# Expert gate and up products in three rounded matmuls, with their weights loaded apart from the down weights

## The chip, the cores and the metric

The kernel runs on one core of a Trainium2 chip. The metric is the time on the device, in microseconds (us), of one execution of the whole program. Engines are named as in the profile: TensorE (PE), ScalarE (ACT), VectorE (DVE), GpSimd (POOL) and SyncE (SP, which here only issues loads).

## The reference

Two transformer blocks over 256 tokens of width 1024, in float32. The first has latent attention, a causal convolution and a mixture of experts; the second has a gated delta rule layer and a forgetting-attention layer. Each layer is modulated by a vector, `ada = silu(c) @ ada_w + ada_b`, whose weights are large. The change touches the mixture of experts:

```python
for gi in range(N_GROUPS):                                   # 4 groups of 8 experts
    a = einsum('td,edf->tef', t, e_gate[gi])                 # d = 1024, f = 128
    u = einsum('td,edf->tef', t, e_up[gi])
    hid = silu(a) * u * combine[:, gi, :, None]              # combine: top 1 group, top 2 experts in it
    out = out + einsum('tef,efd->td', hid, e_down[gi])
```

## The kernel before

Each engine has a program of its own, and they meet at semaphores. `sig(name, events)` declares a semaphore with its events in order; `.then_inc(sig.up(key))` signals one, `e.wait_ge(sig, key)` waits for it.

**Weights** come in chunks, listed in the order of their loads by `chunks()` (L54), most of them 2048 columns of 128 partitions (1 MB). `ring_spots()` (L237) gives each chunk a place in one SBUF tensor, `ring`, of 26624 columns. SP issues the loads strictly in order (`load`, L3290), each after the chunks that lay in its place are freed (`before`, L252, and `freed_by`), and after the chunk eight places earlier in the list is freed. An expert's chunk has 3072 columns: 2048 of gate and up, 1024 of down. Between the experts lie 28 chunks of ada weights.

**The expert stage.** Tokens are routed on DVE (`route`), gathered by group with one-hot matmuls into `xg` (4 groups of 128 columns and a fifth for overflow), and then 40 units run: 32 experts and 8 overflow places, whose weights POOL fetches by indirect loads (`load_over`, L3087). TensorE's loop (from L1501) does in pass u: `up(u)` (L1051: 8 float32 matmuls, 128 tokens stationary, 256 columns of gate and up weights moving), `turn_hid(u-1)` (a transpose), `down(u-2)` (L1067: 2 float32 matmuls of 512 columns), a share of the ada columns, and in half of the passes a scatter of the previous group. The first passes also hold the weighing (`weigh`), the turning of the one-hots (`turn_pick`) and the gathering for the fifth group (`gather_over`). ACT does `silu_up(u)` and copies the transposed result; DVE (loop from L2980) does `gated_up(u)`, then its steps of ada work: each of 14 columns of 512 takes 8 instructions `acc += w[k] * c[k]` over two chunks, in 4 steps; one or two steps a pass,

```python
for _ in range((u + 1) * 7 // 5 - u * 7 // 5):
    next(gad, None)
```

then the scatter's additions to `xT`. POOL is idle in the stage but for the indirect loads, which it starts one after the other as places come free.

**Rounded products.** In most other projections a float32 product is made of three float32r products. A chunk in the list `SPLIT` is split in four pieces of 512 columns: ACT copies each, rounded, to `wH2` (`high`, L1568), and `wL2 = ring - wH2` is computed by POOL (`low`, L3060) or, where `by_dve` (L266) says so, by DVE. Both have two buffers of 2048 columns, so a chunk may be split once the chunk two before it in `SPLIT` was used. `split.need(name)` runs the splits up to that chunk at that point of an engine's program. The matmuls are `three` (L699): high by high, low weights by high, high weights by low. `xH2` and `xL2` hold the split tokens. `wH2`, `wL2`, `xH2` and `xL2` lie over columns 8192 to 20480 of `ring`, which the expert stage uses for chunks.

Of the kernel before, what the change touches and what calls it, by code (L numbers as in the profile page):

```python
# [17 lines left out]
RING = 20480  # L18
LONG = 26624
FIRST = 8192  # L20
LATE = 6144
NLOAD = 8
# [31 lines left out]
def chunks():  # L54
# [47 lines left out]
    for u in range(40):  # L102
        add(f"ex{u}" if u < 32 else f"ov{u - 32}", "expert", None, (0, 3072))
        while h < 28 and 10 * h <= 7 * u + 10:
# [34 lines left out]
def sizes():  # L139

    at, out = 0, {}
    for name, source, rows, cols in chunks():
        if source == "expert":
            out[name] = (0, 3072)
            continue
# [88 lines left out]
SPLIT = [n for n in ORDER if PLACE[n][1] == 2048 and n[:3] != "ada" and n[0] not in "uw"]  # L234


def ring_spots():  # L237
    out, at = {}, 0
    for name in ORDER:
        k = PLACE[name][1]  # L240
        at = {"ada3a": RING, "wob": 0, "ada4a": FIRST, "wout0a": 6144, "wout0b": 0, "ada7a": FIRST, "wout1a": 2048, "ada9a": 16384, "rt": RING + 1024, "ex0": 0, "ada1b": 4096, "ov6": LONG - 3072, "ada2_1_5b": 10240, "ov7": RING}.get(name, at)
        if at + k > (LONG if name in EARLY or "ex4" in out and name in WIDE else RING if name in WIDE else FIRST if "gt3b" not in out else LATE):
            at = 0
        out[name] = (at, at + k)
        at += k
# [6 lines left out]
def before(n):  # L252

    lo, hi = SPOT[ORDER[n]]
    if ORDER[n][:2] == "ov":
        out = [f"ov{int(ORDER[n][2:]) - 4}"] if int(ORDER[n][2:]) > 3 else []
    else:
        out = [m for m in ORDER[n % NLOAD:n:NLOAD] if m[:2] != "ov"][-1:]
# [7 lines left out]
def by_dve(name, q):  # L266

    if name[:2] in ("cv", "in") or name[0] in "ab":
        return q % 2 == 1
# [24 lines left out]
def build_program(nc, ins, out):  # L294
    ctx = ExitStack()
    with ctx:
# [22 lines left out]
        with ExitStack() as part:  # L319
            ring = part.enter_context(nc.sbuf_tensor("ring", [128, LONG], F32))  # L320
# [17 lines left out]
        with ExitStack() as part:  # L338
            sb1("ring_end", [128, LONG - RING])
            xg = sb1("xg", [128, 8, 640])  # L340
# [6 lines left out]
            silu = sb1("silu", [128, 2, 128])  # L347
            hid = sb1("hid", [128, 2, 128])
            hidT = sb1("hidT", [128, 2, 128])
            wsl = sb1("wsl", [128, 40])  # L350
        accs = [sz[:, 2 * i:2 * i + 2, :].rearrange("p i n -> p (i n)") for i in range(2)]
# [136 lines left out]
        norm_h = sig("norm_h", [(u, k) for u in (0, 2, 3) for k in K8])  # L488
# [29 lines left out]
        wo_p, wo_d = sig("wo_p", range(16)), sig("wo_d", range(16))  # L518
        yc_h = sig("yc_h", K8)
# [3 lines left out]
        wu_p = sig("wu_p", K8)  # L523
# [5 lines left out]
        hk_a, hk_d = (sig(n, [(h, q) for h in H2 for q in H2]) for n in ("hk_a", "hk_d"))  # L529
# [2918 lines left out]
```

## Time and profile before

| | us |
|---|---|
| median of 3 runs (lowest, highest) | 1166.06 (1163.05, 1166.13) |
| profiled execution | 1165.98 |
| its span, first to last instruction | 1163.9 |
| TensorE busy | 1091.4 |
| DVE, ACT, POOL busy | 627.6, 485.4, 394.3 |
| mean granted clock of TensorE | 0.975 |
| expert stage, first unit's matmul to last down product | 288.3 to 532 |

The page of the profile gives busy times over the whole span; stretches of it, called windows, are asked for by their start and end in us from the start of the span. Lines such as L687 are those of a helper that issues every matmul, so groups are told apart by their tiles: `bank<-ring,xg` is the gate and up product, `bank<-ring,hidT` the down product, `sz<-ring,cact,sz` an ada accumulation, `wL<-ring,wH` a low piece of a split.

### The profile page before, as it was taken

The page shows a single profiled execution, that of the slowest core. Times are in us where ns is not written, and L with a number is a line of the kernel's source. Part 1 is how long each engine was busy: PE and PEld are TensorE (multiplying, and loading weights), DVE is VectorE, ACT ScalarE, POOL GpSimd, SP SyncE. Part 2 cuts the span into 40 slices and gives each one's busy share as a digit, 9 for nine tenths or more (in the row PEclk, how much of TensorE's full clock was granted, in tenths as well). Part 3 has the DMA queues.
Part 4 walks back from the last instruction along what each step waited for, and adds up shares of the span by engine and source line. Part 5 has one row for each costly group of instructions (what it writes and reads, how often), then busy time and mean ns, then how long its engine had stood idle before and what let it go on. Part 6 is the DMA issues. An engine that isn't in the chain of part 4 may idle for free. (4 is left out here: it accounts for less than half of the span.)

```text
span 1163.9 us, 20437 instructions
## 1 busy us (share of the span) xinstructions
PE 1091.4 (94%) x8310; PEld 930.1 (80%) x8310; DVE 627.6 (54%) x1369; ACT 485.4 (42%) x1091; POOL 394.3 (34%) x337
## 2 busy tenths in 40 slices
PE   5989979999989999999989999999899989999996
PEld 2787778888767777776878889899788878788875
DVE  5789862864425455454654535634554353454473
ACT  3433444304101101104575865746734544465543
POOL 0541342100000000112584563555442436455431
PEclk9999989999999999999999999999999998899999
DMA  9524324587499999604222322232211223233311
GB/s 365 220 104 180 108 74 157 193 361 308 169 381 376 391 394 398 228 14 183 73 109 75 109 74 74 73 110 77 106 38 39 90 94 120 99 109 125 130 37 37
DMA packets 25869, 186.25 MB, mean 160 GB/s; under 512 B 4144, under 2 KB 4912, under 8 KB 5680
## 3 DMA queue, kind: packets, MB, share of 16 engines
q1 hardware_dynamic: 24192, 184.77, 41.5%
q8 instruction: 66, 1.08, 0.4%
q10 hardware_dynamic: 432, 0.18, 0.1%
q14 instruction: 27, 0.22, 0.1%
q0 software_dynamic: 1152, 0.00, 0.1%
HBM read 196.46 MB, written 1.05 MB: 170 GB/s over the span
## 5 line engine op out<-in xcount | busy, mean ns | idle before, releaser
L3058 POOL TENSOR_TENSOR wL<-ring,wH 128x512 fp32r<-128x512 f32 x210 | 277.7, 1336 | 304.9 <-ACT wH L1566 304.4
L687 PE MATMUL bank<-xH,wH 128*128 128x256 f32 x832 | 260.5, 313 | 16.1 <-DVE xL L2195 7.1
L687 PE MATMUL bank<-xH,wL 128*128 128x256 f32 x832 | 240.1, 289 | 0.0
L687 PE MATMUL bank<-xL,wH 128*128 128x256 f32 x832 | 239.8, 288 | 0.0
L687 PEld LDWEIGHTS bank<-xH,wH 128*128 128x128 f32 x832 | 164.0, 197 | 33.3 <-issue 13.7
L687 PEld LDWEIGHTS bank<-xH,wL 128*128 128x128 f32 x832 | 164.5, 198 | 4.9 <-issue 4.3
L687 PEld LDWEIGHTS bank<-xL,wH 128*128 128x128 f32 x832 | 163.9, 197 | 0.0
L1566 ACT ACTIVATE wH<-ring 128x512 fp32r<-128x512 f32 x264 | 154.5, 619 | 8.6 <-PE bank L687 5.4
L687 PE MATMUL bank<-ring,xg 128*128 128x256 f32 x640 | 145.5, 381 | 3.5 <-DMA ring<-in_exw 3.5
L687 PEld LDWEIGHTS bank<-ring,xg 128*128 128x128 f32 x640 | 119.5, 190 | 26.2 <-DMA ring<-in_exw 7.0
L2195 DVE SCALAR_TENSOR_TENSOR sz<-ring,cact,sz 128x512 f32<-128x512 f32 x154 | 118.4, 769 | 4.3
L1566 ACT ACTIVATE arena<-bank 128x512 f32<-128x512 f32 (+5 forms) x133 | 67.3, 511 | 123.8 <-PE bank L687 98.2
L3092 POOL DMA_INDIRECT ring<-in_exw,small x8 | 8.2, 1020 | 275.9 <-DVE sz L2195 242.1
L1563 ACT ACTIVATE silu<-bank 128x128 f32<-128x128 f32 x40 | 11.1, 278 | 199.7 <-PE bank L687 199.7
L687 PE MATMUL bank<-arena 64*64 64x64 f32 (+5 forms) x1056 | 81.7, 252 | 6.2 <-DVE arena L2192 4.9
L2195 DVE SCALAR_TENSOR_TENSOR arena<-bank,vec,arena 128x255 f32<-128x255 f32 (+2 forms) x96 | 46.1, 481 | 66.1 <-ACT arena L1566 63.7
L687 PEld LDWEIGHTS bank<-arena 64*64 64x64 f32 (+4 forms) x1056 | 66.6, 154 | 18.8 <-issue 12.8
L687 PE MATMUL bank<-arena,ring 128*128 128x256 f32 (+2 forms) x336 | 75.5, 381 | 1.5 <-POOL arena L3243 1.2
L2195 DVE SCALAR_TENSOR_TENSOR hid<-silu,wsl,bank 128x128 f32<-128x128 f32 x40 | 13.8, 347 | 115.6 <-ACT silu L1563 110.1
L687 PE MATMUL bank<-ring,hidT 128*128 128x512 f32 x160 | 75.1, 593 | 0.0
L2195 DVE SCALAR_TENSOR_TENSOR arena<-arena,vec 128x256 f32<-128x256 f32 (+1 forms) x132 | 65.9, 566 | 12.9 <-ACT arena L1563 12.9
L687 PEld LDWEIGHTS bank<-arena,ring 128*128 128x128 f32 (+2 forms) x336 | 60.0, 181 | 14.0 <-POOL arena L3243 2.0
(213 smaller groups left out, 1850.5 us busy)
## 6 DMA issues: line engine op xcount, KB each, us to landing
ring<-in_wts SPq DMA_DIRECT2D x123, 1024.0 KB, 5.1
ring<-in_exw SPq DMA_DIRECT2D x32, 1536.0 KB, 9.2
ring<-in_wts SPq DMA_DIRECT2D x1, 1152.0 KB, 5.2
xT<-in_xT SPq DMA_DIRECT2D x1, 1024.0 KB, 13.4
out<-hT SPq DMA_DIRECT2D x4, 256.0 KB, 2.5
cst<-in_cst SPq DMA_DIRECT2D x1, 800.0 KB, 6.3
ring<-in_wts SPq DMA_DIRECT2D x1, 640.0 KB, 3.7
vec<-in_vec SPq DMA_DIRECT2D x1, 217.0 KB, 5.7
```

The source lines that it names most:

```text
L687: return pe.matmul(o, l, r, start=start, stop=stop, skip_group_check=True)
L1563: return act.activation(o, a, func, scale=scale, bias=bias)
L1566: return act.activation(o, a, ACT.Copy, scale=scale)
L2195: return dve.scalar_tensor_tensor(o, a, s, b, op0, op1)
L3058: return pool.tensor_tensor(o, x, h.bitcast(F32), ALU.subtract)
L3092: pool.indirect_dma_start(raw(name)[:, 0, :], None, ins["exw"], bass.IndirectOffsetOnAxis(ap=rowi[:, j:j + 1], axis=0), bounds_check=4095, ...
```

## The change

- `up` uses rounded products: the chunk's two halves by the group's split tokens. The chunk of an expert is cut in two, `ex` (gate and up, 2048 columns) and `dn` (down, 1024 columns). `ex` and `ov` chunks go into `SPLIT`.
- In the list of loads `ex` runs three units ahead of `dn`, and the ada chunks come two to three units later than before.
- In the stage `ring` has four expert places of 3072 columns and two ada places of 2048, outside `wH2` to `xL2`. The first three overflow chunks go over `xg` and what follows it (columns 28672 to 37888).
- A load waits for the chunk twelve places earlier to have landed, no longer for one eight places earlier to be freed.
- ACT and DVE get `group(t, h)`: the high and the low part of half of group t's tokens. The ada steps on TensorE and DVE begin with pass 2.
- POOL runs the splits of the stage, and waits in `load_over` between them. Several semaphores are merged.

```diff
     for u in range(40):
-        add(f"ex{u}" if u < 32 else f"ov{u - 32}", "expert", None, (0, 3072))
-        while h < 28 and 10 * h <= 7 * u + 10:
+        for n in range(3 if u else 0, 4):
+            if u + n < 32:
+                add(f"ex{u + n}", "expert", None, (0, 2048))
+        if u < 32:
+            add(f"dn{u}", "expert", None, (2048, 3072))
+        else:
+            add(f"ov{u - 32}", "expert", None, (0, 3072))
+        while h < 28 and 10 * h <= 7 * u - 3:
...
-SPLIT = [n for n in ORDER if PLACE[n][1] == 2048 and n[:3] != "ada" and n[0] not in "uw"]
+SPLIT = [n for n in ORDER if n[:2] == "ov" or PLACE[n][1] == 2048 and n[:3] != "ada" and n[0] not in "uw"]
+def expert_spots():
+    four = (0, 3072, RING, RING + 3072)
+    out = {f"ex{u}": four[u % 4] for u in range(32)}
+    out.update((f"dn{u}", four[u % 4] + 2048) for u in range(32))
+    out.update((f"ov{j}", (LONG, LONG + 3072, LONG + 6144, *four, LONG)[j]) for j in range(8))
+    for n in ORDER[ORDER.index("rt"):ORDER.index("gqk0a")]:
+        if n[:3] == "ada":
+            out[n] = 6144 if n[-1] == "a" else RING + 6144
+    return {**out, "gqk0a": 0, "gqk0b": 6144, "ba": 2048}
...
 def by_dve(name, q):
-    if name[:2] in ("cv", "in") or name[0] in "ab":
+    if name[:2] == "ex":
+        return q == 3 and name != "ex0"
+    if name[:2] in ("cv", "in", "ov") or name[0] in "ab":
         return q % 2 == 1
...
             def up(u):
-                t, w = u // 8, raw(expert(u))
-                p = bank(u % 2)
-                e.wait_ge(loaded(expert(u)), expert(u))
+                t, name = u // 8, expert(u)
+                wh, wl = parts(name, 8)
+                p = bank(u % 2)[:, 0:256]
+                c = slice(128 * (t % 2), 128 * (t % 2) + 128)
                 for k in range(8):
-                    e.wait_ge(*((xg_a, k) if t < 4 else (pick_a, "o1")))
-                    i = mm(p[:, 0:256], xg[:, k, 128 * t:128 * t + 128], w[:, 0, 256 * k:256 * k + 256], k == 0, k == 7)
+                    e.wait_ge(lo_of(name, k // 2), (name, k // 2))
+                    e.wait_ge(hk_d, ("g", t, k // 4))
+                    mm(p, xH2[:, k, c], wh[:, k, :], k == 0, False)
+                    mm(p, xH2[:, k, c], wl[:, k, :], False, False)
+                    i = mm(p, xL2[:, k, c], wh[:, k, :], False, k == 7)
...
-                for _ in range((u + 1) * 7 // 5 - u * 7 // 5):
+                for _ in range((u - 1) * 7 // 5 - (u - 2) * 7 // 5 if u >= 2 else 0):
                     next(gad, None)
...
+            def group(t, h):
+                if t >= 2:
+                    e.wait_ge(up_p, 8 * t - 9)
+                if t == 4:
+                    e.wait_ge(pick_a, "o1")
+                else:
+                    e.wait_ge(xg_a, 4 * h + 3)
+                s, c = slice(4 * h, 4 * h + 4), 128 * (t % 4)
+                cp(xH2[:, s, 128 * (t % 2):128 * (t % 2) + 128], xg[:, s, c:c + 128]).then_inc(xg_a.up((t, h)))
...
             high_tokens()
+            split.need("ex0")
             gather()
+            group(0, 1)
+            split.need("ex1")
             for u in range(42):
                 if u < 40:
                     silu_up(u)
...
                 if 1 <= u < 41:
                     turn_hid(u - 1)
+                if u < 38:
+                    split.need(f"ex{u + 2}" if u < 30 else f"ov{u - 30}")
+                if u % 8 in (2, 3) and u < 32:
+                    group(u // 8 + 1, u % 8 - 2)
...
             route()
             gad = chain(*[ada(j) for j in range(10, 24)])
+            group(0, 0)
+            group(0, 1)
+            split.need("ex1")
             for u in range(42):
...
                 if 1 <= u < 40:
                     gated_up(u)
-                for _ in range((u + 1) * 7 // 5 - u * 7 // 5):
-                    next(gad, None)
+                if u >= 2:
+                    for _ in range((u - 1) * 7 // 5 - (u - 2) * 7 // 5):
+                        next(gad, None)
+                if u < 38:
+                    split.need(f"ex{u + 2}" if u < 30 else f"ov{u - 30}")
+                if u % 8 in (2, 3) and u < 32:
+                    group(u // 8 + 1, u % 8 - 2)
...
-            e.wait_ge(rt_d, "rowi")
-            for j in range(8):
-                load_over(j)
+            for u in range(40):
+                split.need(f"ex{u}" if u < 32 else f"ov{u - 32}")
+                if u == 28:
+                    e.wait_ge(rt_d, "rowi")
+                    for j in range(3):
+                        load_over(j)
+                if 31 <= u < 36:
+                    load_over(u - 28)
...
+                for m in [m for m in ORDER[n % NLOAD:n:NLOAD] if m[:2] != "ov"][-1:]:
+                    e.wait_ge(loaded(m), m)
                 for m in before(n):
```

## Rows read from the trace of the kernel before

**Rows 1.** The page, part 1: busy us (share of the span) xinstructions.

```profile
PE 1091.4 (94%) x8310; PEld 930.1 (80%) x8310; DVE 627.6 (54%) x1369; ACT 485.4 (42%) x1091; POOL 394.3 (34%) x337
```

**Rows 2.** Windows of the expert stage (first line: columns).

```profile
core 0: us, PE busy (x) PEld busy (x) DVE busy (x) ACT busy (x) POOL busy (x), PEclk, DMA share, GB/s
302.30:367.80 65.50, 61.20 (x279) 45.70 (x278) 25.20 (x45) 8.00 (x27) 0.00 (x0) 1.00 0.86 345
367.80:474.10 106.30, 106.30 (x475) 80.42 (x474) 52.76 (x100) 10.18 (x40) 2.21 (x2) 1.00 0.97 390
474.10:526.70 52.60, 52.60 (x235) 39.81 (x234) 25.58 (x52) 5.09 (x20) 5.95 (x6) 1.00 0.30 104
500.00:520.00 20.00, 20.00 (x93) 15.50 (x92) 9.20 (x19) 1.33 (x6) 3.35 (x4) 1.00 0.02 1
```

**Rows 3.** Waits of TensorE, 296 to 365 us: total, times, longest.

```profile
PE bank L687 <- DMA ring<-in_exw: 3.5, 3, 1.9
```

**Rows 4.** Timeline of TensorE: start us, us, what; the transposes of passes 2 and 39.

```profile
302.28 0.27 PE L691 MATMUL bank<-cst,hid 128*128 128x128 f32 x1
...
526.69 0.27 PE L691 MATMUL bank<-cst,hid 128*128 128x128 f32 x1
```

**Rows 5.** Timeline of TensorE, gate and up products; windows of the last projections.

```profile
288.27 7.07 PE L687 MATMUL bank<-ring,xg 128*128 128x256 f32 x32
967.55:973.30 5.75, 5.75 (x48) 5.75 (x49) 1.02 (x2) 2.34 (x5) 5.75 (x7) 1.00 0.52 184
```

**Rows 6.** Tile ring: duration ns min/median/max; then timelines of POOL and DVE.

```profile
L1566 ACT ACTIVATE wH<-ring x264: 612/617/648, 24.7 to 1146.6; 128x512 fp32r<-128x512 f32 x132
L3058 POOL TENSOR_TENSOR wL<-ring,wH x210: 1252/1289/1791, 25.4 to 1146.5; 128x512 fp32r<-128x512 f32 x105
L2192 DVE TENSOR_TENSOR wL<-ring,wH x54: 674/692/1782, 28.3 to 1147.2; 128x512 fp32r<-128x512 f32 x54
...
31.54 3.38 POOL L3058 TENSOR_TENSOR wL<-ring,wH 128x512 fp32r<-128x512 f32 x2 [1.42 <-ACT wH L1566]
31.38 4.09 DVE L2192 TENSOR_TENSOR wL<-ring,wH 128x512 fp32r<-128x512 f32 x3
...
539.08 2.35 DVE L2192 TENSOR_TENSOR wL<-ring,wH 128x512 fp32r<-128x512 f32 x2
```

**Rows 7.** Groups of DVE, 367.8 to 474.1 us: busy us, mean ns.

```profile
L2195 DVE SCALAR_TENSOR_TENSOR sz<-ring,cact,sz 128x512 f32<-128x512 f32 x45 | 33.7, 750 | 1.2
L2195 DVE SCALAR_TENSOR_TENSOR xT<-bank,adaT,xT 128x256 f32<-128x256 f32 x20 | 8.7, 478 | 1.9 <-PE bank L687 1.7
L2198 DVE TENSOR_SCALAR sz<-ring,cact 128x512 f32<-128x512 f32 x7 | 3.4, 480 | 0.0
```

**Rows 8.** DMA, 368 to 474 us.

```profile
DMA packets 4671, 41.41 MB, mean 391 GB/s; under 512 B 772, under 2 KB 772, under 8 KB 772
q1 hardware_dynamic: 4388, 41.33, 96.8%
```

**Rows 9.** Timelines of DVE and TensorE at the start of the stage.

```profile
293.05 0.48 DVE L2198 TENSOR_SCALAR sz<-ring,cact 128x512 f32<-128x512 f32 x1
295.17 2.29 PE L687 MATMUL bank<-small,pick 128*128 128x8 f32 x20
298.22 0.33 PE L691 MATMUL bank<-cst,hid 128*128 128x128 f32 x1 [0.76 <-DVE hid L2195]
```

**Rows 10.** Windows, columns as in rows 2.

```profile
536.00:539.30 3.30, 1.71 (x11) 1.10 (x10) 3.25 (x9) 3.30 (x8) 3.30 (x4) 1.00 0.00 0
539.40:542.80 3.40, 3.40 (x8) 2.70 (x9) 2.03 (x2) 1.18 (x4) 3.40 (x3) 0.50 0.51 173
```

**Rows 11.** Timelines at the end of the stage; the page, part 6: KB, us to landing.

```profile
527.47 1.53 DVE L2195 SCALAR_TENSOR_TENSOR sz<-ring,cact,sz 128x512 f32<-128x512 f32 x2
534.66 4.27 ACT L1566 ACTIVATE wH<-ring 128x512 fp32r<-128x512 f32 x8
535.03 0.36 PE L687 MATMUL bank<-pickT,ysH 128*128 128x256 f32 x1
...
ring<-in_wts SPq DMA_DIRECT2D x123, 1024.0 KB, 5.1
```

More of the change, by code:

```diff
@@ L18 @@
 RING = 20480
-LONG = 26624
+LONG = 28672
+OVER = 37888
 FIRST = 8192
 LATE = 6144
-NLOAD = 8
+NLOAD = 12
 BIG = 1.0e30
@@ L143, in sizes @@
         if source == "expert":
-            out[name] = (0, 3072)
+            out[name] = (0, cols[0][1] - cols[0][0])
             continue
@@ L254, in before @@
     lo, hi = SPOT[ORDER[n]]
[L255 to L258, printed above, removed]
+    out = []
     for m in range(n - 1, max(-1, n - 40), -1):
@@ L319, in build_program @@
         with ExitStack() as part:
-            ring = part.enter_context(nc.sbuf_tensor("ring", [128, LONG], F32))
+            ring = part.enter_context(nc.sbuf_tensor("ring", [128, OVER], F32))
         sb("ring_start", [128, LATE])
@@ L487, in build_program @@
         norm_a = sig("norm_a", [(u, k) for u in G4 for k in K8])
-        norm_h = sig("norm_h", [(u, k) for u in (0, 2, 3) for k in K8])
+        norm_h = sig("norm_h", [(u, k) for u in range(4) for k in K8])
         hi_a = sig("hi_a", [(n, q) for n in SPLIT for q in G4])
@@ L528, in build_program @@
         hk_p = sig("hk_p", H2)
-        hk_a, hk_d = (sig(n, [(h, q) for h in H2 for q in H2]) for n in ("hk_a", "hk_d"))
+        hk_a = sig("hk_a", [(h, q) for h in H2 for q in H2])
+        hk_d = sig("hk_d", [(h, q) for h in H2 for q in H2] + [("g", t, h) for t in range(5) for h in H2])
         rt_p, rt_d = sig("rt_p", ["lg", "rank"]), sig("rt_d", STEPS)
@@ L598, in ada_name @@
             return f"ada{j}" if j < 12 else f"ada2_{j // 6 - 2}_{j % 6}"
-        def under_split():
-            names = [n for n in WIDE if SPOT[n][0] < RING and 12288 < SPOT[n][1]]
-            return [freed_by([n for n in names if (n[:3] == "ada") == x][-1])[0] for x in (False, True)]
         def used(name):
             x = 2 * (name[-1] == "b") + 1
+            if name[:2] in ("ex", "ov"):
+                return up_p, int(name[2:]) + 32 * (name[0] == "o")
             if name[:2] == "cv":
@@ L647, in ahead @@
                 for _ in range(n):
-                    if i < len(SPLIT) and self.n < 4 * i + 4 and SPLIT[i][:4] != "gqk0":
+                    if i < len(SPLIT) and self.n < 4 * i + 4 and SPLIT[i][:2] not in ("ex", "ov") and SPLIT[i][:4] != "gqk0":
                         self.go()
@@ L1026, in gather_over @@
                 m.then_inc(pick_p.up(f"o{i}"))
-                until(7, (pick_a, f"o{i}"))
+                until(2, (pick_a, f"o{i}"))
             def weigh():
@@ L1067, in down @@
             def down(u):
-                t, w = u // 8, raw(expert(u))
+                t, name = u // 8, f"dn{u}" if u < 32 else f"ov{u - 32}"
+                w = raw(name)[:, 0, -1024:]
+                e.wait_ge(loaded(name), name)
                 e.wait_ge(ht_a, u)
```

119 lines of the change are left out of this document (66 added, 53 removed).

## The prediction, made before the changed kernel was run

> **What bounds the kernel now.** I read the page first, then the stage of the experts by windows, then its engines one by one. TensorE is busy for 94% of the span [rows 1], so the page alone says that TensorE bounds the kernel. The expert stage runs from 288 to about 533 us. In its middle TensorE was busy for all 106.3 us, at full clock, and the DMA engines for 0.97 of it, while POOL had nothing to do but two gathers [rows 2]. Two limits therefore lie on top of each other. Only in the first 65.5 us did TensorE wait: 4.3 us were not busy, of which 3.5 us were waits for expert weights [rows 2, 3].
>
> The stage has a simple clock. In pass u TensorE does the gate and up products of unit u, the transpose for unit u-1, the down product of unit u-2, then a share of the ada columns and of the scatter. The transpose's one matmul marks the pass: the marks at 302.28 and 526.69 [rows 4] are passes 2 and 39, and the windows of rows 2 are cut at such marks: 10 passes in 65.5 us, 18 in 106.3 (5.91 each), 9 in 52.6.
>
> **The products.** A unit's gate and up product is 8 float32 matmuls of 256 columns, recorded as 16; 32 of them take 7.07 us, less the tail of the last (0.17), so 0.216 us each and 3.45 a unit [rows 5]. The change makes 24 float32r matmuls of 256 columns. The trace has the same shape in the last projections: 48 in 5.75 us, 0.12 us each [rows 5], so 2.88 a unit. TensorE gains 0.576 us a pass, 5.8 in the first ten, 10.4 in the middle 18 and 5.2 in the last 9. I take this as firm.
>
> **What must now be made.** Each unit's 2048 columns are rounded by ACT in four pieces of 0.617 us (2.5 a unit, and ACT is 10% busy) and subtracted in four pieces: three on POOL (1.289 each, 3.9 a unit), one on DVE (0.692 at the median) [rows 2, 6]. For the eight overflow units it is two and two. The token halves cost an ACT and a DVE instruction of 512 elements for each half of each group of 8 units, ten in all. DVE's own work in the middle 18 passes is 52.8 us [rows 2], of which 45 accumulations and 7 first products of ada columns, all with SBUF sources, are 37.1 and the scatter's additions, from PSUM, 8.7 [rows 7]. It grows by 18 x 0.69 = 12.4 and some 4.5 x 0.69 = 3.1, to 68.3 us. That would hide in 95.9 us of TensorE if DVE and POOL did not disturb each other.
>
> They do. Where both subtract back to back, POOL's two took 3.38 us and DVE's three 4.09; at 539 us DVE's two took 2.35 [rows 6]. A pair in turns costs about 1.7 us, against 1.29 and 0.69 alone. So a POOL instruction holds up DVE by between 0 (DVE is idle or works from PSUM just then) and 1.0 us (1.7 - 0.69). With 54 of them in 18 passes DVE needs between 68.3 and 122 us. I take 0.6, since DVE's accumulations come in runs of two or four inside POOL's run of three but scatter and gating work lies between: 68.3 + 32.4 = 100.7 us.
>
> The Trainium skill (SBUF — State Buffer, "SBUF: two separate sides") calls the pair of ports that DVE and GpSimd share an exclusive lock, held for the whole instruction, against a DVE instruction with two SBUF inputs. By that rule a pair costs the sum of both, 1.98 us, and the middle passes at least 54 x 1.289 plus 37.1 of ada work plus 15.5 of new subtractions, 122 us: an estimate that falls on the far end of my range. The trace agrees that the two hinder each other, but its pairs take 1.7 us, less than the rule gives [rows 6].
>
> **DMA.** The 18 passes moved 41.41 MB at 391 GB/s with the queue at 96.8% [rows 8]. At 100% that is 41.41/0.404 = 102.5 us for the same weights. The change moves the same bytes, so this too ends the middle part later than TensorE (95.9). The smaller ring (four expert places and two ada places, 16384 columns instead of 26624) is covered as long as a chunk may be late by some 10 us: an expert's chunk is free once it is split, two passes ahead of its use, instead of after the down product.
>
> So the middle part: the last of 95.9 (TensorE), 100.7 (DVE) and 102.5 (DMA): 102.5, a gain of 3.8 where TensorE alone would give 10.4. The first ten passes have little ada and scatter work; there TensorE's 5.8 and the 3.5 of waits come off, 9.3 together, since gate and up chunks are now asked for before the stage begins instead of after the first down product. In the last nine DMA is no limit (104 GB/s [rows 2]); DVE's need is 25.6 + 16 x 0.69 + 16 x 0.6 = 46.2 us of 47.4 left by TensorE. POOL now waits there for down products ahead of its splits, and each overflow load costs it about 1 us (5.95 for six [rows 2]). I take 4.5 of the 5.2.
>
> **What the change adds at the start.** Unit 0 used to begin at 288.27, beside DVE's routing. Now it waits for the low halves of the tokens, which DVE subtracts only after its routing ended at 293.05 [rows 9]: begin at 294.0 (one subtraction and two semaphores), units 0 and 1 in 5.8, to 299.8. The weighing (20 small matmuls from 295.17, then 0.8 of waiting until 298.22 [rows 9]) takes 3.05 as before, to 302.9, and unit 2 ends at 305.8 instead of 301.8: +4.0. Bounds: 2.5, if DVE is let off earlier, and 5.5. TensorE idles for 5.7 us meanwhile. At 536 to 539.3 it was busy for 1.71 of 3.3 us, and then ran 3.4 us at 0.50 of its clock, 1.2 GHz [rows 10]. I add such a stretch, 1.7 us; bounds 0 and 3.4.
>
> **At the end.** The ada steps begin two passes later. Before, two steps (four accumulations, the first two from 527.47 in 1.53 us) followed the last gating; now five do, 7.7 us, and the last chunk is only asked for when its place is freed in the first of them, 5.1 us before it lands [rows 11]. The last group's low half, and with it the last scatter (535.03 [rows 11]), is late by the three steps more less some 2.3 us in which DVE used to idle there (2.3), or by the landing and two steps (4.3). The splits for the next projection (534.66, 4.27 us of ACT) wait for a load from the same queue. I take 3.0.
>
> Costed at nothing: the merged semaphores, the wait for a landing in place of a freeing among the early loads (it lets some ada chunks come sooner, but DVE there waits ahead of other work that TensorE paces), unit 0's own split (5.2 us of POOL, which is idle then, beside the gather; without that cover unit 0 would begin that much later, but it has to wait for DVE until 294 anyway), and the overflow loads, which transfer nothing here (two of them ran at 500 to 520 us, where DMA moved 1 GB/s [rows 2]).
>
> **Sum**, against the profiled execution's 1165.98 us (span 1163.9 and 2.1 around it; the median of the runs shown, 1166.06, is the same): +4.0 +1.7 -9.3 -3.8 -4.5 +3.0 = -8.9, so 1157 us.
>
> **Rivals.**
> - A, TensorE keeps its pace. Chunks loaded ahead cushion DMA and DVE slips between POOL's instructions: 5.7 - 9.3 - 10.4 - 5.2 + 2.3 = -16.9, 1149 us. For it: DVE has 30 us of room if POOL costs it nothing, and POOL itself needs only 3.9 us a pass. Against it: DMA at 0.97 [rows 2]. Chance 0.25.
> - B, slower: DVE and POOL in turns bound the stage. If each POOL instruction costs DVE 1.0, the middle takes 122.2 us (+15.9), the first ten 25.2 + 8.4 + 30 = 63.6 (-1.9), the last nine 52.5 (-0.1); with start and end 5.7 + 4.3 that is +23.9, 1190 us. The forecast turns into it at about 0.75 us a POOL instruction, where the whole change is worth nothing. For it: the pairs of rows 6, and that ada accumulations come back to back. By the Trainium skill's rule of the lock (SBUF — State Buffer, as above) the middle would take about the same. Chance 0.27.
> - C, the smaller ring starves the queue. A stuck ada load holds SP, and behind it the experts' loads: at 90% of the queue's time instead of 96.8% the middle takes 114 us, +7.7 instead of -3.8: about +3, 1169 us. For it: an ada chunk waits for DVE to free one two chunks back. Against it: expert chunks have two passes of room. Chance 0.1.
> - That nothing changes because the new products don't run is excluded: 24 matmuls replace 16 in every unit.
>
> The forecast's own case has 0.38; its range with start, end and DVE's 0.5 to 0.7 is 1151 to 1164.
>
> **How the numbers follow.** A measurement tells about 0.3% (3.5 us) of this kernel from no change. Faster: all of A, 0.28 of the forecast's 0.38 and little of C, 0.54. Same: 0.07 of the forecast, 0.05 of B, 0.03 of C, 0.15. Slower: the rest, 0.31. The range goes from A's value less the clock's 1.7 (1147) to B at 0.9 us a POOL instruction (1180); B's far end is left out.
>
> **What would show it.** Right: matmuls of 0.12 us in the stage, marks of 5.7 us in the middle with the DMA share at 0.95 or more, POOL at some 70%, TensorE idle from 288.3 to 294, no wait for expert loads before 345 us. If DVE's accumulations average over 1.1 us and TensorE waits for DVE's low pieces or gating, B holds; if marks are 5.3 us, A; if the DMA share falls while SP waits for an ada place, C. The prediction is wrong at its root if the stage is paced by something with no term here, such as ACT waiting ahead of the splits.

## The result: 1.7% slower, and where the profile shows it

The changed kernel took 1184.91 us at the median of four runs (1183.32 to 1186.62) beside 1165.72 for the kernel before: a ratio of 1.017 (95% interval 1.0149 to 1.0191), 19 us more. The forecast was 1157, with a range up to 1180. The profiled execution has a span of 1183.5 us.

The same windows, cut at the same marks, carry the reading. Part 1 of the page after the change, then the timeline of TensorE at the transposes of passes 2, 28, 29, 30 and 39 ("start us, us, what"):

```profile
PE 1080.0 (91%) x8630; PEld 933.7 (79%) x8630; DVE 743.5 (63%) x1426; ACT 574.3 (49%) x1261; POOL 566.0 (48%) x450
...
316.53 0.27 PE L708 MATMUL bank<-cst,tmpb 128*128 128x128 f32 x1
...
467.52 0.30 PE L708 MATMUL bank<-cst,tmpb 128*128 128x128 f32 x1
...
481.71 0.41 PE L708 MATMUL bank<-cst,tmpb 128*128 128x128 f32 x1
...
487.92 0.27 PE L708 MATMUL bank<-cst,tmpb 128*128 128x128 f32 x1
...
543.25 0.27 PE L708 MATMUL bank<-cst,tmpb 128*128 128x128 f32 x1
```

The windows of the changed kernel, with the columns of [rows 2]: ten passes, eighteen, nine.

```profile
316.50:375.90 59.40, 55.30 (x359) 45.05 (x358) 53.07 (x53) 31.03 (x71) 49.05 (x31) 1.00 0.86 336
375.90:487.90 112.00, 99.70 (x611) 80.06 (x610) 100.35 (x123) 50.66 (x116) 86.80 (x58) 0.97 0.89 353
487.90:543.20 55.30, 49.53 (x307) 40.31 (x306) 52.98 (x72) 21.57 (x52) 28.07 (x21) 0.97 0.40 144
```

| part | before | after | forecast | found |
|---|---|---|---|---|
| to the mark of pass 2 | 302.3 | 316.5 | +5.7 | +14.2 |
| first ten passes | 65.5 | 59.4 | -9.3 | -6.1 |
| middle 18 | 106.3 | 112.0 | -3.8 | +5.7 |
| last nine | 52.6 | 55.3 | -4.5 | +2.7 |
| the rest | 637.2 | 640.3 | +3.0 | +3.1 |

TensorE does less work (PE 1080.0 against 1091.4 [rows 1]) and waits more. In [rows 2] it was busy for all 106.3 us of the middle, now for 99.7 of 112. DVE rose from 52.8 to 100.4 us and POOL from 2.2 to 86.8. The groups of DVE and POOL in the middle passes (busy us, mean ns) say what DVE's time is:

```profile
L2237 DVE SCALAR_TENSOR_TENSOR sz<-ring,cact,sz 128x512 f32<-128x512 f32 x46 | 55.9, 1215 | 1.2
L2234 DVE TENSOR_TENSOR wL<-ring,wH 128x512 fp32r<-128x512 f32 x18 | 23.2, 1287 | 0.0
L2237 DVE SCALAR_TENSOR_TENSOR xT<-bank,adaT,xT 128x256 f32<-128x256 f32 x20 | 8.7, 472 | 0.0
...
L3114 POOL TENSOR_TENSOR wL<-ring,wH 128x512 fp32r<-128x512 f32 x55 | 85.1, 1576 | 17.9 <-ACT wH L1589 17.9
```

The accumulation that took 750 ns [rows 7] takes 1215 on average, DVE's subtraction 1287 against 692 at the median [rows 6], POOL's 1576 against 1289. The scatter's addition, which reads one operand from PSUM, stayed at 472 ns (478 before). This is rival B's sign ("over 1.1 us"), and so are TensorE's waits between 300 and 545 us, for DVE's pieces (`wL`), its token halves (`xL`) and its gating (`tmpb`), and once for POOL's (total, times, longest):

```profile
PE bank L704 <- DVE wL L2234: 11.3, 8, 2.7
PE bank L704 <- DVE xL L2234: 8.3, 1, 8.3
PE bank L704 <- POOL wL L3114: 6.4, 1, 6.4
PE bank L708 <- DVE tmpb L2237: 3.5, 4, 1.9
```

The loss isn't an even pace. From transpose to transpose, 14 of the middle 18 passes of the changed kernel are as short as in e9_dve below, where TensorE alone sets the pace, or longer by 0.9 us at most. Passes 17, 20 and 22 lost 6.3 us together, and pass 28 alone 8.9 (14.2 against 5.3).

**The start.** First two groups of DVE's routing in the kernel before: eight masks, and three additions. Then timelines of the changed kernel: the same masks and POOL beside them, the same additions and POOL, and TensorE's first gather product.

```profile
279.15 1.66 DVE L2198 TENSOR_SCALAR pick<-cst,small 128x128 fp32r<-128x128 f32 x8
290.77 0.46 DVE L2192 TENSOR_TENSOR small<-small 128x2 f32<-128x2 f32 x3
...
279.38 4.82 DVE L2240 TENSOR_SCALAR pick<-cst,small 128x128 fp32r<-128x128 f32 x8
...
278.38 4.95 POOL L3114 TENSOR_TENSOR wL<-ring,wH 128x512 fp32r<-128x512 f32 x4 [43.94 <-ACT wH L1589]
...
296.71 2.23 DVE L2234 TENSOR_TENSOR small<-small 128x2 f32<-128x2 f32 x3
...
295.19 3.72 POOL L3114 TENSOR_TENSOR wL<-ring,wH 128x512 fp32r<-128x512 f32 x3 [11.86 <-ACT wH L1589]
...
284.29 0.77 PE L704 MATMUL bank<-pick,hkH 128*128 128x512 f32 x1 [3.32 <-issue]
```

The eight masks that the gather needs take 4.8 us instead of 1.7 beside POOL's four pieces of unit 0, and three additions of two elements per partition take 2.2 us instead of 0.5 beside those of unit 1. The routing is on the path now, because unit 0 waits for the token halves behind it: this is the wait of 8.3 us above. The granted clock of the gather in the kernel before (first line), then in the changed kernel that of the gather, the idle time, and unit 0's and 1's products:

```profile
280.90:288.20 7.30, 7.29 (x32) 6.07 (x33) 1.81 (x11) 4.29 (x8) 0.00 (x0) 1.00 0.73 305
...
284.20:292.95 8.75, 8.66 (x32) 6.99 (x32) 1.77 (x12) 4.74 (x9) 0.00 (x0) 0.82 0.82 312
292.95:301.55 8.60, 0.35 (x2) 0.00 (x0) 7.88 (x29) 4.66 (x8) 3.72 (x3) 0.77 0.00 0
301.55:308.70 7.15, 7.11 (x49) 7.14 (x49) 1.39 (x3) 2.36 (x5) 1.80 (x2) 0.79 0.65 229
```

**Single stalls.** POOL's timeline around the longest wait in the middle passes (6.4 us, for POOL's pieces):

```profile
471.20 1.21 POOL L3154 DMA_INDIRECT ring<-in_exw,small  x1 [6.62 <-issue]
472.71 0.99 POOL L3154 DMA_INDIRECT ring<-in_exw,small  x1 [0.30 <-issue]
474.01 1.06 POOL L3154 DMA_INDIRECT ring<-in_exw,small  x1 [0.30 <-issue]
475.09 2.51 POOL L3114 TENSOR_TENSOR wL<-ring,wH 128x512 fp32r<-128x512 f32 x2
```

Three overflow loads stand ahead of unit 29's pieces. By the code they first wait for the low token halves of group 4, because they overwrite the gathered tokens; DVE finished those at 470.1, and POOL issued at 471.2.

### The profile page after: what moved, and what is told of

It is laid out like the page before. It is cut to its first block and busy times, and to the rows that moved or that the text cites. A ratio compares the mean times of both kernels' runs of the same rounds, so it can differ in the third digit from the quotient of the medians.

```text
span 1183.5 us, 21606 instructions
## 1 busy us (share of the span) xinstructions
PE 1080.0 (91%) x8630; PEld 933.7 (79%) x8630; DVE 743.5 (63%) x1426; ACT 574.3 (49%) x1261; POOL 566.0 (48%) x450
## 3 DMA queue, kind: packets, MB, share of 16 engines
q0 software_dynamic: 1152, 0.00, 0.1%
## 5 line engine op out<-in xcount | busy, mean ns | idle before, releaser
L3114 POOL TENSOR_TENSOR wL<-ring,wH 128x512 fp32r<-128x512 f32 x323 | 448.4, 1407 | 409.5 <-ACT wH L1589 409.0
L1589 ACT ACTIVATE wH<-ring 128x512 fp32r<-128x512 f32 x424 | 242.0, 621 | 18.5 <-DMA ring<-in_exw 10.1
L704 PEld LDWEIGHTS bank<-xH,wH 128*128 128x128 f32 x832 | 164.6, 198 | 33.3 <-issue 14.2
L2237 DVE SCALAR_TENSOR_TENSOR sz<-ring,cact,sz 128x512 f32<-128x512 f32 x154 | 154.0, 1000 | 6.6 <-DMA ring<-in_wts 2.2
L704 PE MATMUL bank<-wH,xH 128*128 128x256 f32 x384 | 120.5, 314 | 26.0 <-DVE wL L2234 11.3
L2234 DVE TENSOR_TENSOR wL<-ring,wH 128x512 fp32r<-128x512 f32 x101 | 109.7, 1096 | 34.5 <-ACT wH L1589 34.1
L704 PE MATMUL bank<-wH,xL 128*128 128x256 f32 x384 | 112.4, 293 | 0.0
L704 PE MATMUL bank<-wL,xH 128*128 128x256 f32 x384 | 112.3, 292 | 0.0
L704 PEld LDWEIGHTS bank<-wH,xH 128*128 128x128 f32 x384 | 77.7, 202 | 31.8 <-DVE wL L2234 13.1
L704 PEld LDWEIGHTS bank<-wL,xH 128*128 128x128 f32 x384 | 77.6, 202 | 3.3 <-issue 3.3
L1586 ACT ACTIVATE tmpb<-bank 128x128 f32<-128x128 f32 (+1 forms) x48 | 15.8, 330 | 131.5 <-PE bank L704 131.5
L704 PEld LDWEIGHTS bank<-wH,xL 128*128 128x128 f32 x384 | 77.4, 202 | 0.0
```

Source lines behind the costliest of these rows:

```text
L704: return pe.matmul(o, l, r, start=start, stop=stop, skip_group_check=True)
L1586: return act.activation(o, a, func, scale=scale, bias=bias)
L1589: return act.activation(o, a, ACT.Copy, scale=scale)
L2234: return dve.tensor_tensor(o, a, b, op)
L2237: return dve.scalar_tensor_tensor(o, a, s, b, op0, op1)
L3114: return pool.tensor_tensor(o, x, h.bitcast(F32), ALU.subtract)
```

## The experiments

Ratios are to the kernel before on the same chip (its median 1165.1, 1166.0 and 1165.9 us in the three sets).

| run | us | ratio (95%) | pass 2 | ten | eighteen | nine | rest |
|---|---|---|---|---|---|---|---|
| changed kernel | 1184.9 | 1.0170 (1.0149 to 1.0191) | 316.5 | 59.4 | 112.0 | 55.3 | 640.3 |
| e1_start | 1176.0 | 1.0085 (1.006 to 1.011) | 307.1 | 60.8 | 111.5 | 56.4 | 639.9 |
| e2_over | 1175.9 | 1.0070 (1.0039 to 1.0100) | 318.5 | 58.8 | 107.0 | 53.2 | 640.0 |
| e3_thin | 1160.5 | 0.9960 (0.9943 to 0.9978) | 316.4 | 56.1 | 99.6 | 47.4 | 638.0 |
| e4_ring | 1162.6 | 0.9975 (0.9956 to 0.9994) | 300.6 | 62.0 | 105.1 | 52.6 | 638.4 |
| e5_both | 1164.7 | 1.0001 (0.9978 to 1.0023) | 307.8 | 60.9 | 108.8 | 47.4 | 638.0 |
| e7_mix | 1157.7 | 0.9929 (0.9905 to 0.9953) | 300.2 | 62.1 | 100.0 | 52.7 | 640.4 |
| e8_mixd | 1151.0 | 0.9892 (0.984 to 0.9945) | 302.2 | 56.6 | 100.0 | 52.8 | 635.1 |
| e9_dve | 1154.0 | 0.9910 (0.9886 to 0.9933) | 308.0 | 56.1 | 95.1 | 53.2 | 638.9 |
| e10_best | 1144.4 | 0.9813 (0.9778 to 0.9848) | 301.8 | 56.1 | 95.0 | 52.0 | 640.8 |
| e11_twice | 1233.7 | 1.058 (1.0543 to 1.0618) | 310.8 | 76.8 | 147.5 | 55.8 | 642.5 |
| e12_lead | 1150.2 | 0.9854 (0.9815 to 0.9892) | 301.4 | 58.9 | 95.7 | 56.2 | 636.1 |

**e1_start: the routing without POOL's pieces beside it.**

```diff
             for u in range(40):        # POOL
+                if u < 2:
+                    e.wait_ge(rt_d, ("ed", "rowi")[u])
                 split.need(f"ex{u}" if u < 32 else f"ov{u - 32}")
```

> The changed kernel, but POOL waits before its four low pieces of unit 0 until DVE has made the routing's first masks and sums, and before its three pieces of unit 1 until DVE's routing has ended. Theory H (POOL's subtractions hold DVE's small routing instructions): the first gather product comes 3.4 us sooner, at 281 us, the routing ends near 293.5 instead of 301, unit 0's products begin near 294 instead of 301.6, the mark of pass 2 comes near 308 instead of 316.5, and the time falls by 8 to 9 us, to about 1176. Rival (unit 0 is late for another reason: ACT's copies of the gathered tokens, or the ring's new order): DVE's routing runs undisturbed, but unit 0 begins no sooner than 299, and the time stays within 3 us of 1185; if POOL's later pieces of unit 1 are what is late next, units 1 and 2 wait for them and 3 to 5 us come back.

Two rows of TensorE's timeline: the first gather product and the first of unit 0.

```profile
279.18 0.47 PE L704 MATMUL bank<-pick,hkH 128*128 128x512 f32 x1 [0.17 <-issue]
...
292.16 0.55 PE L704 MATMUL bank<-wH,xH 128*128 128x256 f32 x1 [5.45 <-DVE xL L2234]
```

It came out as theory H had it: 1176, with each mark one to two microseconds earlier than expected. From the first gather product to the mark of pass 2 it is 27.9 us, where the kernel before took 21.4 and the changed one 32.2. The 6.5 us that remain are the wait for DVE and the lower clock after it (PEclk 0.79 from 292.1 to 307.1 us), which the forecast had priced at 5.7 together.

**e2_over: the overflow loads one at a time.**

```diff
-                if u == 28:
-                    e.wait_ge(rt_d, "rowi")
-                    for j in range(3):
-                        load_over(j)
-                if 31 <= u < 36:
-                    load_over(u - 28)
+                if u == 30:
+                    e.wait_ge(rt_d, "rowi")
+                if 30 <= u < 38:
+                    load_over(u - 30)
```

> The changed kernel, but POOL issues the eight overflow loads one after each of its turns 30 to 37, instead of three together after turn 28 (ahead of the low pieces of unit 29) and five after turns 31 to 35, where each waits for a down product. Theory H (what stalls the passes at 469 to 476 and 501 to 523 us is POOL standing in these loads ahead of its subtractions, and DVE held meanwhile): the wait of 6.7 us for POOL's pieces goes, and of the three waits of 1.7 to 3.0 us in the last nine passes at least two; the time falls by 9 to 13 us, to 1172 to 1176. Rival B (the pace of DVE and POOL in turns bounds these passes anyway): the waits only move, under 4 us fall. Rival C (the smaller ring): nothing changes, 1185.

The middle fell by 5.0 and the last nine by 2.1, 7.1 us together in the profiled executions; by the medians it is 9.0 us in all, and the runs scatter more than most (1170.3 to 1179.3). The wait of 6.4 us is gone and one of the three late ones is left. The middle is still 0.7 us above the kernel before, though TensorE has 10 us less to do.

**e3_thin: POOL's pieces cut to 64 columns.**

```diff
-                            c = slice(512 * q, 512 * q + 512)
+                            c = slice(512 * q, 512 * q + (64 if name[:2] in ("ex", "ov") and name not in ("ex0", "ex1") else 512))
```

> The changed kernel, but from unit 2 on POOL subtracts only 64 of the 512 columns of each of its pieces (the other low columns of gate and up weights are left as the units before left them, so three quarters of the low product of these units isn't computed; instructions, waits and loads are the same in number). It prices what POOL's subtractions cost the rest. Theory B or H (they hold DVE): DVE's accumulations of ada columns fall from 1215 to about 750 ns, the 18 middle passes from 112.0 us to between 95.9 (TensorE alone) and 102.5 (the weights' transfer at the queue's full rate), the ten before them from 59.4 to about 56.5, the last nine from 55.3 to about 50; the start stays. Time about 1167. If the middle ends near 102.5 with the DMA share above 0.95, the forecast's floor was right and only its price for POOL wrong; near 96, rival A's pace was open to it. Theory C (ring and order bound the stage): the middle stays above 108 us, with the DMA share at 0.9 and the queue waiting for ada places, and the time falls by less than 7 us.

```profile
316.40:372.50 56.10, 54.73 (x359) 44.90 (x358) 34.12 (x58) 30.97 (x71) 13.72 (x30) 1.00 0.89 354
372.50:472.10 99.60, 96.37 (x612) 78.98 (x611) 65.90 (x120) 49.67 (x116) 30.34 (x57) 0.98 0.98 400
472.10:519.50 47.40, 47.40 (x308) 38.81 (x307) 36.31 (x68) 21.56 (x52) 13.23 (x21) 1.00 0.44 159
...
L2237 DVE SCALAR_TENSOR_TENSOR sz<-ring,cact,sz 128x512 f32<-128x512 f32 x44 | 33.4, 759 | 2.8 <-DMA ring<-in_wts 1.8
```

The windows are the run's three parts, the last line DVE's accumulations in the middle. These are back at 759 ns and the middle ends at 99.6 us. Of that, 3.2 us is still the wait behind the overflow loads, so the passes themselves take 96.4: close to TensorE's own 95.9, and below the 102.5 that the forecast took for the transfer's floor. All of it comes from the work of POOL's subtractions, whose number stayed the same. The time, 1160.5, is below the 1167 expected, since TensorE reached its own pace in the middle and in the last nine.

**e4_ring: the ring and the order alone.** All forty units go to a float32 branch of `up`; nothing of the experts is split, and a gate and up chunk is freed by its product.

```diff
+RAW = [f"ex{u}" for u in range(32)] + [f"ov{j}" for j in range(8)]
-SPLIT = [n for n in ORDER if n[:2] == "ov" or PLACE[n][1] == 2048 and n[:3] != "ada" and n[0] not in "uw"]
+SPLIT = [n for n in ORDER if n not in RAW and (n[:2] == "ov" or PLACE[n][1] == 2048 and n[:3] != "ada" and n[0] not in "uw")]
...
+                if name in RAW:
+                    e.wait_ge(loaded(name), name)
+                    c = slice(128 * (t % 4), 128 * (t % 4) + 128)
+                    for k in range(8):
+                        e.wait_ge(*((xg_a, k) if t < 4 else (pick_a, "o1")))
+                        i = mm(p, xg[:, k, c], raw(name)[:, 0, 256 * k:256 * k + 256], k == 0, k == 7)
```

> The changed kernel's ring and order alone: gate and up chunks three units ahead of the down chunks, four expert places and two ada places, ada steps two passes later, but the products of all forty units from the loaded weights in float32 as before, with no rounding and no subtraction of weights (the overflow units stand in other places, since the gathered tokens are now read until the last unit; the token halves are still made, and read by nobody). Theory H or B: the start is as before the change (pass 2 near 302.3), the passes take about 65, 106.3 and 52.6 us, the tail 3 us more than before: 1167 to 1170. Theory C (the small ring starves the queue, since an ada load stuck behind DVE holds the experts' loads): the middle takes 112 us or more although nothing is subtracted, and the time is 1175 or more.

The ratio is 0.9975: the new ring starves nothing, which ends theory C. It gains 2.9 us. The first ten passes take 62.0 instead of 65.5, the 3.5 us of waits for expert weights [rows 3] being gone. The expected 1167 to 1170 had kept these waits, and so was missed.

**e5_both: e1 and e2 together.**

> The changed kernel with both holds of the two runs before taken away: POOL's pieces of units 0 and 1 held back behind the routing's steps, and the overflow loads one after each of POOL's turns 30 to 37. Theory H (separate losses, each POOL standing in DVE's or its own way): they add, 9.0 + 9.0 us less than the changed kernel: 1167, with pass 2 near 308, the middle 18 passes 106 to 107 us, the last nine 53. What is left against the other runs is the pace of DVE and POOL in turns: DVE busy for over 0.95 of the middle passes. Rival (one loss is hidden behind the other, or the stage's end waits for ada chunks and DVE anyway): 1172 or more.

```profile
307.80:368.70 60.90, 56.68 (x359) 45.88 (x358) 53.63 (x53) 31.07 (x71) 47.95 (x31) 0.97 0.84 332
368.70:477.50 108.80, 99.54 (x613) 78.45 (x611) 106.85 (x124) 50.99 (x116) 89.39 (x57) 0.98 0.92 365
477.50:524.90 47.40, 47.40 (x308) 38.80 (x307) 46.05 (x71) 21.57 (x52) 32.22 (x22) 1.00 0.47 168
```

The two losses add: 1164.7 us, a ratio of 1.0001. What remains is the pace. DVE is busy for 106.9 of 108.8 us, and the three rounded products are worth nothing to the whole.

**e9_dve: e5 with every piece from unit 2 to 31 on DVE.**

```diff
-        return q == 3 and name != "ex0"
+        return name not in ("ex0", "ex1") or q == 3 and name == "ex1"
```

> The kernel with both holds taken away, but from unit 2 on DVE subtracts all four pieces of each unit (the overflow units' stay two and two): POOL subtracts nothing in the first 28 passes of the stage. DVE's own work in the middle 18 passes is then 54.1 + 18 x 4 x 0.69 + 5 x 0.69 = 107.2 us at undisturbed durations. Theory B (a POOL piece costs DVE about as much as subtracting it itself, since they take turns): accumulations at 750 ns, pieces at 690, the middle 106 to 109 us, the time within 3 us of the kernel with both holds taken away, though POOL's work is gone. Rival (POOL's pieces hold DVE little, and offload it as they were meant to): the middle 112 us or more, the time 5 to 10 us longer.

Windows of the first two parts, then DVE's pieces in the middle (busy us, mean ns):

```profile
308.00:364.10 56.10, 54.73 (x358) 44.88 (x357) 49.60 (x85) 31.06 (x71) 0.00 (x0) 1.00 0.93 364
364.10:459.20 95.10, 95.09 (x613) 77.69 (x612) 92.34 (x171) 50.09 (x116) 2.99 (x2) 1.00 1.00 410
...
L2234 DVE TENSOR_TENSOR wL<-ring,wH 128x512 fp32r<-128x512 f32 x69 | 43.0, 686 | 0.0
```

Neither theory had this: 10.7 us faster than e5. With 50 more subtractions DVE is busy for 92.3 us, 14.5 less than with POOL's help. The expectation's 107.2 counted 0.69 us for each piece, which was too much. Back to back, pieces start 0.60 us apart (three of them take 1.89 us in a row of e11_twice below), because the records overlap at their ends, and 69 x 0.60 = 41. Counted so, DVE's other work is 92.3 - 41.4 = 50.9. In e5 its busy time less 19 own pieces (11.4), less that work and less three accumulations more in its window (2.2) leaves 42.4 us for 55 pieces of POOL: **0.77 us each, more than the 0.60 it costs DVE to do the piece itself**. This is an estimate: it takes DVE's records to overlap in e5 as they do in e9.

**e7_mix and e8_mixd: half the units split, with POOL and without** (the second edit is e8_mixd's alone).

```diff
+RAW = ["ex0", "ex1"] + [f"ex{u}" for u in range(11, 32, 2)] + [f"ov{j}" for j in range(8)]
...
-        return q == 3 and name != "ex0"
+        return name not in ("ex0", "ex1") or q == 3 and name == "ex1"
```

> The changed kernel's ring, but units 0 and 1, every odd unit from 11 and the overflow units multiply the loaded weights in float32 as before the change; units 2 to 10 and the even ones from 12 to 30 are split as in the change (three pieces on POOL, one on DVE). The overflow units stand in other places and are loaded one after each of POOL's turns 30 to 37. From the run of the ring alone (span 1158.7; 61.9, 105.2 and 52.6 us for the three parts): TensorE saves 9 x 0.576 = 5.2 us in the first part, 5.2 in the middle, 0.6 in the last. Theory B with H: POOL's 27 pieces in the middle cost DVE at most 27 us on 63, so it isn't the bound there, and the middle takes 100 us; the first part has all its units split and takes 57 to 59. Time 1152 to 1154. Rival (any mixing of POOL and DVE stalls single passes, since pieces come late): parts of 60 and 104, 1158.

> The same mixture of units (0, 1, odd ones from 11 and the overflow units in float32, the others split), but DVE subtracts all pieces and POOL none. DVE needs 27.2 + 9 x 2.77 = 52 us in the first part and 54.1 + 9 x 2.77 + 3.5 = 82.5 in the middle. Theory B with H: nothing takes turns with it, TensorE is the bound everywhere: 56.7, 100 and 52 us, time 1151 to 1153, the fastest of all that compute everything. Rival (DVE's pieces, queued behind its waits for ada chunks and for gating, come late, so that POOL would have been the better place): slower than the run with POOL's pieces by 2 us or more.

With POOL's pieces the first ten passes take 62.1 us, with one wait of 3.7 us for a piece of DVE's; without them 56.6. In the middle both take 100.0, since TensorE has 5.2 us more to do there and is the bound. e7 missed its 1152 to 1154 by the first part, where nine units of ten are split. Its 1157.7 is the rival's 1158, but not by the rival's parts (60 and 104). e8 hit its range at 1151.0. The two give the price a second time: their middle windows hold the same DVE instructions but for the 27 pieces that POOL does in e7, and DVE is busy for 79.5 us in e7 and 75.3 in e8. So 27 pieces on POOL cost it 4.2 + 27 x 0.60 = 20.4 us, 0.75 each.

**e11_twice: POOL busy with work of nobody's.** e9_dve, and POOL subtracts constants besides.

```diff
+                for q in range(3 if 2 <= u < 32 else 0):
+                    e.wait_ge(hi_a, (f"ex{u}", q))
+                    if (u, q) != (2, 0):
+                        e.wait_ge(twice, (u, q - 1) if q else (u - 1, 2))
+                    pool.tensor_tensor(sqn[:, :], cst[:, 512:1024], cst[:, 0:512], ALU.subtract).then_inc(twice.up((u, q)))
```

> The kernel in which DVE subtracts all pieces from unit 2 on (1154 us), and POOL besides makes three subtractions of 512 columns a unit for units 2 to 31, from constants into a tile that nobody reads in this stage: what the kernel computes stays the same, only POOL is busy. It prices POOL's subtractions by themselves, on tensors that DVE doesn't touch. Theory B (the two engines take turns at their access to the memory, whatever tensors they read, and each POOL subtraction costs DVE 0.8 us, the value that follows from the two runs with the pieces on either engine): the middle grows from 95.1 to 92.3 + 54 x 0.8 = 135 us, the first part from 56 to about 74, and the time to about 1212; with 0.6 as in the forecast the middle is 125. Rival (the hold comes from both working on the same weights and rounded halves, or from waits on each other's semaphores): accumulations stay at 750 ns, the middle at 95 to 97, the time at 1154 to 1157.

The middle window; DVE's two groups and POOL's one in it; a row of DVE's timeline with POOL idle and one with POOL busy; POOL's row beside the latter.

```profile
387.60:535.10 147.50, 115.97 (x612) 91.99 (x612) 146.44 (x176) 49.95 (x117) 84.23 (x56) 0.87 0.67 264
...
L2236 DVE TENSOR_TENSOR wL<-ring,wH 128x512 fp32r<-128x512 f32 x72 | 78.4, 1148 | 0.0
L2239 DVE SCALAR_TENSOR_TENSOR sz<-ring,cact,sz 128x512 f32<-128x512 f32 x44 | 48.1, 1094 | 1.1
...
L3316 POOL TENSOR_TENSOR sqn<-cst 128x512 f32<-128x512 f32 x54 | 81.7, 1514 | 62.2 <-ACT wH L1590 56.6
...
423.12 1.89 DVE L2236 TENSOR_TENSOR wL<-ring,wH 128x512 fp32r<-128x512 f32 x3
...
424.33 2.39 DVE L2236 TENSOR_TENSOR wL<-ring,wH 128x512 fp32r<-128x512 f32 x2
...
424.47 3.40 POOL L3316 TENSOR_TENSOR sqn<-cst 128x512 f32<-128x512 f32 x2 [5.50 <-ACT wH L1590]
```

DVE's busy time went from 92.3 to 146.4 us with 54 subtractions on POOL that touch none of its tensors. Less the three pieces, one accumulation and one first product more in this window (3.0 us), that is 0.95 us each. So the hold is between the engines and not between the data, and the rival (shared tensors, semaphores) falls. The time, 1233.7, is beyond the 1212 expected with 0.8.

**e10_best: the version that follows.** RAW is `["ex0", "ex1"]` and the overflow units; units 2 to 31 are split with all pieces on DVE.

> The changed kernel's ring; units 0 and 1 and the overflow units multiply the loaded weights in float32, all units from 2 to 31 are split, every piece of theirs on DVE, none on POOL; overflow loads one after each of POOL's turns 30 to 37. Put together from the marks of the runs before: start as in the mixture (pass 2 near 302), first part 56.1 and middle 95.1 us as where DVE subtracted everything, last nine 52.8 less 2 x 0.576 = 51.7, tail 635 to 640. Theory B with H: 1143 to 1148, faster than both kernels and than every run so far. Rival (DVE, at 0.97 of the middle passes, has no room, so that its backlog shows as waits in the last nine passes as it did there, 53.2 with three waits): last nine 53 to 55, 1149 or more.

```profile
301.80:357.90 56.10, 54.73 (x359) 44.88 (x357) 49.59 (x87) 30.98 (x70) 1.33 (x1) 1.00 1.01 414
357.90:452.90 95.00, 94.98 (x611) 77.56 (x610) 92.06 (x170) 49.97 (x116) 0.00 (x0) 1.00 1.00 411
452.90:504.90 52.00, 52.00 (x243) 39.73 (x242) 30.16 (x60) 5.09 (x20) 7.27 (x7) 1.00 0.46 162
```

1144.4 us, a ratio of 0.9813: 21 us faster than the kernel before, 40 than the changed one. Units 0 and 1 need no token halves, so the start is that of before; every later pass is TensorE's. DMA is at 1.00 and DVE at 0.97 of the middle as well, so three limits now lie close together.

**e12_lead: e10 with the ada steps two passes earlier again.**

```diff
-        while h < 28 and 10 * h <= 7 * u - 3:
+        while h < 28 and 10 * h <= 7 * u + 10:
...
-                if u >= 2:
-                    for _ in range((u - 1) * 7 // 5 - (u - 2) * 7 // 5):
-                        next(gad, None)
+                for _ in range((u + 1) * 7 // 5 - u * 7 // 5):
+                    next(gad, None)
```

> The first kernel of these three, with the ada chunks loaded and their steps made two passes earlier, as before the change. The forecast's term for the tail (three more ada steps after the last gating, the last chunk asked for late): the tail falls by 2 to 4 us, the time too, to 1141 to 1144. Rival (the tail is set by something else, such as the ada load that waits for DVE in either order, or the splits for the next projection): the tail stays within 1 us; if the earlier ada loads delay the experts' first chunks, the first part grows by what the tail gains.

The rest of the kernel took 4.7 us less, a little more than expected, but the ten passes took 2.8 more and the last nine 4.2 more, of which 2.2 was a wait of TensorE for an overflow load and 1.1, in the first part, one for an accumulation. In all it is slower (1150.2 against 1144.4) and misses its 1141 to 1144: the later ada steps buy more than they cost. The rest of the kernel scatters between 635.1 and 642.5 us in the runs with the later order, so its 4.7 us alone would show nothing. The last scatter does: its first product comes 8.3 us after the transpose of pass 39 in the kernel before and here, and 11.3 to 12.3 us after it in all the others, so the tail term is real at that point. By the first product of the next projection less of it is left: 26.5 us after the same mark in these two, 27.1 to 29.3 in the others.

## Why the prediction was wrong, step by step

- **The sum's form held.** The parts, their marks and rival B's signs were named in advance, and the profile after shows B's. B's own 1190 was nearer than the forecast, and came with other parts.
- **Three steps failed.** Two terms were "costed at nothing", POOL's early pieces and the overflow loads: without both losses the kernel takes 1164.7 us instead of 1184.9 (e5_both), so they cost 20.2. The third is the price "I take 0.6", with the 7.7 us that e5_both still lies above 1157.
- **"I take 0.6".** A piece on POOL cost DVE 0.77 us in e5_both, 0.75 in e7_mix, and 0.95 in e11_twice. The bound of 1.0 from the pairs of [rows 6] held, and the break-even of 0.75 was right: at 0.77, with the other two losses gone, the change is worth a ratio of 1.0001. In the changed kernel itself DVE's busy time in the middle, 100.4 us, is the forecast's 100.7, but it sat idle for 6.7 us in pass 28; where that stall is gone (e5_both) it needs 106.9, and the middle takes 108.8 instead of 102.5. And waits came in single passes before DVE's time was full: in the first ten of e5_both it was busy for 53.6 of 60.9 us. The reason given for 0.6, scatter and gating between the runs of pieces, covers only the little DVE work that reads PSUM (8.7 and 6.0 us in the middle).
- **"Unit 0's own split ... which is idle then"** looked at POOL and not at DVE beside it. The gather began 3.4 us later than before (284.3 against 280.9) and took 1.4 longer (8.7 against 7.3 us busy, PEclk 0.82 against 1.00), and the routing lost 3 more beside unit 1's pieces. So unit 0 began at 301.6 instead of the forecast's 294.0. From there to the mark of pass 2 it is 15.0 us where the forecast had 14.0, so that the missing 8.5 is 7.6 ahead of unit 0 and 1.0 behind it. e1_start gave back 9.0 and left 6.5 where 5.7 stood in the sum.
- **"The overflow loads, which transfer nothing here"** were costed by their bytes. They wait, and the subtractions queue behind them: 9.0 us in e2_over by the medians, 7.1 by its windows. The text had priced a load at 1 us of POOL, about as measured (1.0 to 1.2 in the row of stalls above), but not the wait ahead of it, nor the place in front of unit 29's pieces. The kernel before had such waits too, 4.3 to 15.8 us ahead of the loads from 499 to 517 us, but nothing stood behind them.
- **The DMA floor of 102.5 us was no floor.** The forecast divided the middle window's bytes by the queue's share. The middle passes of e10_best took 95.0 us at 411 GB/s and moved 38.97 MB, not 41.41. At the forecast's 404 GB/s that is 96.5 us, so most of the difference is bytes that moved elsewhere: the first part carried 23.2 MB instead of 22.6 in 9.4 us less, its share rising from 0.86 [rows 2] to 1.01, and the last nine passes 8.4 instead of 5.5, since the ada chunks come later. Had POOL's pieces cost nothing, rival A's pace was open in all three parts, as e3_thin shows (56.1, 96.4 without the overflow wait, 47.4).
- **What was right:** the products' 0.576 us a pass (95.1 in the middle of e9_dve where 95.9 was said), the waits for weights that go (e4_ring: 3.5 us), C's small chance, and the tail's 3.0 as far as the last scatter (11.4 us behind the mark instead of 8.3). That the whole rest came out 3.1 longer is partly luck: at the next projection 0.6 was left (27.1 against 26.5).

The Trainium skill (Perfetto Trace Analysis, "Optimizing Scalar/DVE Operations") warns that moving operations between GpSimd and DVE might not help, because they share a port. The trace agrees and goes further: it hurts, 0.77 us against 0.60. By the lock that the Trainium skill describes (SBUF — State Buffer, "SBUF: two separate sides") the loser is blocked for the whole instruction, which would be 1.29 us here. The cost measured is 0.75 to 0.95. Records of both engines overlap at their ends, so some of the difference may be that; it wasn't tried by itself.

## What to carry to other kernels

Price a subtraction on POOL by what it does to DVE, at its worst row, and compare it with DVE doing the work itself: here DVE alone was the faster place for the stage's pieces. (The other projections kept their pieces on POOL in every run, so for them it isn't shown.) Before giving an idle engine work, look at what the other engines do at that very time, above all short instructions that a chain waits for. And take a queue's busy share for a limit only over all of the stretch in which its transfers could have been made. Last, add up the work of an engine by passes and not only by parts: in the first ten passes of e5_both DVE was busy for 0.88 of the time, and two of them still took 3.4 and 1.3 us longer than in e9_dve.

## What the runs showed of the hardware

- The hold needs no common tensor: 54 subtractions of constants on POOL made DVE's accumulations 1094 ns instead of 751, its pieces 1148 instead of 686 (e11_twice against e9_dve).
- Size doesn't protect: DVE additions of two elements per partition took 0.7 us each beside POOL (three in 2.23 us, 0.46 before), and masks with a single SBUF tensor as input 0.60 us on average (eight in 4.82, 1.66 before). DVE instructions with an operand in PSUM kept their time (472 ns against 478).
- One DVE instruction can be held over two of POOL's. In the changed kernel two pieces took 4.06 us beside an indirect load and two subtractions of POOL, and one of the two pieces 3.46 of it:

```profile
502.02 4.06 DVE L2234 TENSOR_TENSOR wL<-ring,wH 128x512 fp32r<-128x512 f32 x2
...
501.47 1.52 POOL L3154 DMA_INDIRECT ring<-in_exw,small  x1 [2.02 <-PE bank L704]
503.02 2.50 POOL L3114 TENSOR_TENSOR wL<-ring,wH 128x512 fp32r<-128x512 f32 x2
```

- The queue ran at 411 to 414 GB/s over 151 us of e10_best with its share at 1.00 to 1.01, above the 404 at which the forecast put it full.
